# Token tile by token tile in the last two parts of four products, and mask matmuls ahead of the weighted products

## The reference

```python
# block 1: forgetting attention (8 heads), stick-breaking attention, a mixture of 16 experts
# block 2, layer 0:
m = concat(y_conv, y_mla) @ a_w_out                        # "aout"
x = x + rms_norm(m, norm_mix_post[0])
h = rms_norm(x, norm_mlp_pre[0])
x = x + rms_norm(relu(h @ w1[0])**2 @ w2[0], norm_mlp_post[0])   # "up0", "down0"
# block 2, layer 1: attention with 16 heads (compressed, selected, window branches)
m = mixer_c(rms_norm(x, norm_mix_pre[1]))                  # "cin", attention, "cout"
x = x + rms_norm(m, norm_mix_post[1])
x = x + rms_norm(relu(h @ w1[1])**2 @ w2[1], norm_mlp_post[1])   # "up1", "down1"
return x
```

## Time and profile before

| what | value |
|---|---|
| median of 3 runs | 2326.39 us (2326.12 to 2327.95) |
| the profiled execution's own time | 2325.24 us |
| its span | 2323.4 us |
| mean granted TensorE clock | 0.971 |
| TensorE matmul busy | 2192.1 us, 94% |
| VectorE busy / ScalarE busy | 1249.9 us, 54% / 942.8 us, 41% |
| chain that ended last | PE 83%, DVE 8%, DMA 4%, ACT 3%, issue 2% |
| joins: stretches | 1147.8 to 1171 (aout), 1509 to 1533 (down0), 1941 to 1965 (cout), 2303 to 2323.4 (down1) |
| first attention loop / second | 130 to 178 / 1684 to 1903 |

### The profile page before, as it was taken

How to read it: one execution, slowest core, us unless ns; L and a number is a source line. 1 busy time by engine, 2 the same in 40 slices (tenths; PEclk the granted TensorE clock), 3 DMA queues, 4 the chain that set the end, 5 groups by cost and what they waited for, 6 DMA issues and landing times.

```text
span 2323.4 us, 25971 instructions
## 1 busy us (share of the span) xinstructions
PE 2192.1 (94%) x10216; PEld 1689.6 (73%) x10216; DVE 1249.9 (54%) x1719; ACT 942.8 (41%) x1464; POOL 183.2 (8%) x228
## 2 busy tenths in 40 slices
PE   7999999979999968998999999989999998999998
PEld 4767678857666636886778888878766667888886
DVE  6745564468677735366554444453346666344444
ACT  4444542246555524335431134342255555112333
POOL 1230000202000010001000000020222200000000
PEclk9999999999999988999999999999899999999999
DMA  9404023939999972220232232242100002332231
GB/s 352 142 14 157 25 103 132 387 111 343 357 370 376 377 253 99 82 87 15 73 97 94 91 102 98 91 114 88 39 1 1 1 20 73 102 107 91 91 109 55
DMA packets 142951, 308.92 MB, mean 133 GB/s; under 512 B 12438, under 2 KB 14123, under 8 KB 142829
## 3 DMA queue, kind: packets, MB, share of 16 engines
q1 hardware_dynamic: 120484, 229.75, 28.8%
q0 software_dynamic: 11648, 41.60, 4.6%
q10 hardware_dynamic: 10700, 35.91, 4.5%
HBM read 276.04 MB, written 30.99 MB: 132 GB/s over the span
## 4 chain that ended last, share of the span: by engine, by line
PE 83%; DVE 8%; DMA 4%; ACT 3%; issue 2%; ACTq 0%; POOLq 0%; POOL 0%; SPq 0%; DVEq 0%
PE PB L1648 57%; PE PB L2134 5%; PE PB L2418 4%; DMA BIG<-in_expert_w_down 3%; PE PB L2390 1%; PE PB L2391 1%; DVE WL L2521 1%; PE PB L1797 1%; PE PB L1895 1%; PE PB L1776 1%; PE PB L2339 1%; PE PB L2365 1%; PE PB L2074 1%; DVE X L2581 1%; PE PB L1965 1%
## 5 line engine op out<-in xcount | busy, mean ns | idle before, releaser
L2521 DVE TENSOR_TENSOR WL<-RING,WH 128x1024 fp32r<-128x1024 f32 x232 | 288.4, 1243 | 622.6 <-ACT WH L920 400.5
L920 ACT CAST WH<-RING 128x1024 fp32r<-128x1024 f32 x232 | 243.5, 1050 | 792.9 <-PE PB L1648 786.6
L1648 PE MATMUL PB<-HTH,WH 128*128 128x512 f32 x1056 | 413.7, 392 | 8.7 <-DVE WL L2521 3.4
L1648 PE MATMUL PB<-HTL,WH 128*128 128x512 f32 x1056 | 412.4, 391 | 0.0
L1648 PE MATMUL PB<-HTH,WL 128*128 128x512 f32 x1056 | 412.1, 390 | 0.0
L1648 PEld LDWEIGHTS PB<-HTH,WH 128*128 128x128 f32 x1056 | 199.1, 189 | 52.5 <-issue 9.6
L1648 PEld LDWEIGHTS PB<-HTH,WL 128*128 128x128 f32 x1056 | 199.1, 189 | 41.8
L1648 PEld LDWEIGHTS PB<-HTL,WH 128*128 128x128 f32 x1056 | 199.4, 189 | 40.9
L1648 PE MATMUL PB<-WH,NHH 128*128 128x512 f32 x512 | 199.4, 389 | 1.8 <-DVE NHL L2524 1.8
L1648 PE MATMUL PB<-WL,NHH 128*128 128x512 f32 x512 | 199.2, 389 | 0.0
L1648 PE MATMUL PB<-WH,NHL 128*128 128x512 f32 x512 | 199.2, 389 | 0.0
(11 more groups left out here) (559 smaller groups left out, 3527.8 us busy)
## 6 DMA issues: line engine op xcount, KB each, us to landing
RING<-in_mlp_w SPq DMA_DIRECT2D x64, 1024.0 KB, 5.1
RING<-in_expert_w_gate SPq DMA_DIRECT2D x32, 1024.0 KB, 7.6
RING<-in_expert_w_up SPq DMA_DIRECT2D x32, 1024.0 KB, 11.9
BIG<-in_expert_w_down ACTq DMA_DIRECT2D x15, 2048.0 KB
RING<-in_w_in SPq DMA_DIRECT2D x20, 1024.0 KB, 5.5
BIG<-in_ada_w SPq DMA_DIRECT2D x9, 2048.0 KB, 14.7
dispatch_rows<-BIG POOLq DMA_DIRECT2D x24, 512.0 KB, 18.7
RING<-in_a_w_in SPq DMA_DIRECT2D x10, 1024.0 KB, 5.0
```

Source lines behind the costliest of these rows:

```text
L920: ins = nc.scalar.copy(weight_buffers(stage)[0][:, q % 2], halves_of(n, q))
L1648: yield pe.matmul(dst, lhs, rhs, start=(start and n == 0), stop=(stop_ and n == 2))
L2521: ins = V.tensor_tensor(wl, halves_of(n, q), wh.bitcast(F32), ALU.subtract)
```

## The change

- The last part of the four products gets buffers of its own (`LAST_BUFFERS`, in memory that is free then), so ScalarE no longer waits with its high half until the part before has begun. The parity of the weight buffers of up0 and down0 is turned (`W_PARITY`).
- The last two parts of the second group run tile by tile: tile b takes part 6 (or 30) and part 7 (or 31), 12 matmuls, then tile b+1. The last part's operands are waited for at tile 0.
- In the join, ScalarE squares row i-1 of `X` right behind the bank of tile i, and VectorE does for tile i the multiply, the reciprocal and the `X` update, and then the normed row of tile i-1. For down0 the normed rows go to `XN`, since the last parts' rows lie in the memory of `NAT`.
- In both attention loops the maximum masks stand right behind the score mask, ahead of the spread, the transposition of maxima and the weighted product.

```diff
--- before.py
+++ after.py
@@ -783,6 +783,14 @@
 
         BUFFERS = {"down0": (NHH, NHL), "down1": (NHH, NHL), "aout": (HTL[:, 0:4, :], HTL[:, 4:8, :])}
 
+        LAST_PART = {"aout": 7, "cout": 7, "down0": 31, "down1": 31}
+        W_PARITY = {"up0": 1, "down0": 1}
+        LAST_BUFFERS = {
+            "aout": over("LASTA", ht_at, [P, 4, 2, W], F32R), "cout": over("LASTC", big_at + 4096 * F, [P, 4, 2, W], F32R),
+            "down0": over("LASTD", htl_at, [P, 4, 2, W], F32R)}
+        LAST_BUFFERS["down1"] = LAST_BUFFERS["down0"]
+        JOINED = {"aout": NAT, "cout": NAT, "down0": XN}
+
         def weight_buffers(stage):
 
             return (CWH, CWL) if stage == "cout" else (WH, WL)
@@ -791,6 +799,18 @@
         def input_buffers(stage):
 
             return BUFFERS[stage] if stage in BUFFERS else (HTH, HTL)
+
+        def split_weights(stage, q):
+
+            if q == LAST_PART.get(stage):
+                return LAST_BUFFERS[stage][:, 0], LAST_BUFFERS[stage][:, 1]
+            return tuple(t[:, (q + W_PARITY.get(stage, 0)) % 2] for t in weight_buffers(stage))
+
+        def split_rows(stage, q):
+
+            if q == LAST_PART.get(stage):
+                return LAST_BUFFERS[stage][:, 2], LAST_BUFFERS[stage][:, 3]
+            return tuple(tiles_of(t, q % 2) for t in input_buffers(stage))
 
         INPUTS = {
             "wout": lambda q: tiles_of(MT, q % 4), "cout": lambda q: tiles_of(OTS[q % 4 // 2], q % 2),
@@ -883,12 +903,18 @@
                     nc.scalar.activation(SQ512, PB[4 + i][:, :], ACT.Square, accum_out=SSB[:, one]).then_inc(n_sq, 1)
                     act.wait_ge(n_sq, 2 * NT * k + NT + i + 1)
                     nc.scalar.activation(PRMS[:, one], SSB[:, one], ACT.Sqrt, bias=MSA[:, one], scale=1.0 / D).then_inc(p_rms, 1)
-                for i in range(NT if rows_again else 0):
-                    one = slice(i, i + 1)
-                    row_tiles[0] += 1
-                    act.wait_ge(x_rows, row_tiles[0])
-                    link(nc.scalar.activation(SQ1024, X[:, i, :], ACT.Square, accum_out=SS[:, one]))
-                    nc.scalar.activation(RMS[:, one], SS[:, one], ACT.Sqrt, bias=EPSC, scale=1.0 / D).then_inc(n_rms, 1)
+                    if rows_again and i > 0:
+                        row_squares(i - 1)
+                if rows_again:
+                    row_squares(NT - 1)
+
+            def row_squares(i):
+
+                one = slice(i, i + 1)
+                row_tiles[0] += 1
+                act.wait_ge(x_rows, row_tiles[0])
+                link(nc.scalar.activation(SQ1024, X[:, i, :], ACT.Square, accum_out=SS[:, one]))
+                nc.scalar.activation(RMS[:, one], SS[:, one], ACT.Sqrt, bias=EPSC, scale=1.0 / D).then_inc(n_rms, 1)
 
             row_tiles = [0]
 
@@ -915,14 +941,14 @@
 
                 act.wait_ge(arrived[n % SLOTS], slot_count(n, turn, chunks_a_turn))
 
-                if SPLIT[stage] + q > 1 and (stage, q) != ("aout", 1):
+                if SPLIT[stage] + q > 1 and (stage, q) != ("aout", 1) and q != LAST_PART.get(stage):
                     act.wait_ge(part_begun, part_no(stage, q, turn, parts_a_turn))
-                ins = nc.scalar.copy(weight_buffers(stage)[0][:, q % 2], halves_of(n, q))
+                ins = nc.scalar.copy(split_weights(stage, q)[0], halves_of(n, q))
                 if stage in INPUTS:
                     if stage in ("down0", "down1"):
                         m = GR["up" + stage[-1]] + q % 16 // 2
                         act.wait_ge(acc_free[m % 2], m // 2 + 1)
-                    ins = nc.scalar.copy(input_buffers(stage)[0][:, 2 * (q % 2):2 * (q % 2) + 2, :], INPUTS[stage](q))
+                    ins = nc.scalar.copy(split_rows(stage, q)[0], INPUTS[stage](q))
                 ins.then_inc(high_ready, 1)
 
             def evac(g, dst, func=ACT.Copy, scale=1.0, banks=4, width=T):
@@ -1650,14 +1676,15 @@
             def split_group(g, stage, q0, kind, parts=4, wait_norm=None, midway=None, midway_at=2, by_bank=False):
 
                 await_set(g)
-                x = input_buffers(stage)
-                for m in range(parts):
+                tail = by_bank and stage in LAST_PART
+                for m in range(parts - 2 if tail else parts):
                     q = q0 + m
                     pe.wait_ge(low_ready, part_no(stage, q) + 1)
-                    w = tuple(t[:, q % 2] for t in weight_buffers(stage))
+                    w = split_weights(stage, q)
+                    x = split_rows(stage, q) if kind == "D" else input_buffers(stage)
                     for b in range(4):
                         for k in range(2):
-                            kk = 2 * (q % 2) + k if kind == "D" else 2 * m + k
+                            kk = k if kind == "D" else 2 * m + k
                             if wait_norm is not None and (b == 0 or m == 0 and k == 0):
 
                                 pe.wait_ge(norm_low, wait_norm - ND + max(kk, b) + 1)
@@ -1672,7 +1699,27 @@
                             ins.then_inc(bank_done, 1)
                     if midway is not None and m == midway_at:
                         midway()
+                if tail:
+                    ins = last_parts_by_bank(g, stage, q0 + parts - 2)
                 ins.then_inc(acc_done, 1)
+
+            def last_parts_by_bank(g, stage, q0):
+
+                for b in range(NT):
+                    for q in (q0, q0 + 1):
+                        if b == 0:
+                            pe.wait_ge(low_ready, part_no(stage, q) + 1)
+                        w, x = split_weights(stage, q), split_rows(stage, q)
+                        for k in range(2):
+                            for n, ins in enumerate(three(PB[4 * (g % 2) + b][:, :], w, k, x, k, "D",
+                                                          slice(b * P, (b + 1) * P), False, q > q0 and k == 1)):
+                                if b == 0 and k == 0 and n == 0:
+                                    ins.then_inc(part_begun, 1)
+                                if b == 0 and k == 0 and n == 1 and q == q0:
+                                    begin(ins, None)
+                    if b < NT - 1:
+                        ins.then_inc(bank_done, 1)
+                return ins
 
 
             pe.sem_inc(acc_done, GR["mod"])
...
@@ -2447,14 +2494,14 @@
                             pe.wait_ge(q_ready, h + 3)
                         maxima(h + 2, *MAX_TURNS[t])
                     score_mask(n)
+                    if h + 2 < NSA_H and t < len(MAX_TURNS):
+                        max_masks(h + 2, *MAX_TURNS[t])
                     if h % 2 and h >= 3 and t in (1, 3, 5):
                         spread((h - 3) // 2, t // 2)
                     if h + 2 < NSA_H and t == PER_HEAD - 1:
                         max_T(h + 2)
                 if n >= 2:
                     weighted(n - 2)
-                if h + 2 < NSA_H and t < len(MAX_TURNS):
-                    max_masks(h + 2, *MAX_TURNS[t])
 
             def last_pair():
 
@@ -2517,11 +2564,11 @@
             def split(stage, q, n, turn, parts_a_turn, chunks_a_turn):
 
                 dve.wait_ge(high_ready, part_no(stage, q, turn, parts_a_turn) + 1)
-                wh, wl = (t[:, q % 2] for t in weight_buffers(stage))
+                wh, wl = split_weights(stage, q)
                 ins = V.tensor_tensor(wl, halves_of(n, q), wh.bitcast(F32), ALU.subtract)
                 if stage in INPUTS:
-                    rows, (high, low) = slice(2 * (q % 2), 2 * (q % 2) + 2), input_buffers(stage)
-                    ins = V.tensor_tensor(low[:, rows, :], INPUTS[stage](q), high[:, rows, :].bitcast(F32), ALU.subtract)
+                    high, low = split_rows(stage, q)
+                    ins = V.tensor_tensor(low, INPUTS[stage](q), high.bitcast(F32), ALU.subtract)
                 ins.then_inc(low_ready, 1)
 
             def normed_rows():
@@ -2564,28 +2611,31 @@
             def join(stage, rows_again=True):
 
                 k = POST.index(stage)
-                for i in range(NT + 3):
-                    if i < NT:
-                        dve.wait_ge(n_sq, 2 * NT * k + NT + i + 1)
-                        ins = V.tensor_tensor(MN[stage][:, i, W:D], PB[4 + i][:, :], ROW[:, W:D], ALU.mult)
-                        if i == NT - 1:
-                            ins.then_inc(acc_free[1], 1)
-                        else:
-                            link(ins)
-                    if 0 < i <= NT:
-                        one = slice(i - 1, i)
-                        dve.wait_ge(p_rms, NT * k + i)
-                        if i == NT:
-                            dve.wait_ge(acc_free[1], (GR[stage] + 1) // 2 + 1)
-                        link(V.reciprocal(PRSTD[:, one], PRMS[:, one]))
-                        V.scalar_tensor_tensor(out=X[:, i - 1, :], in0=MN[stage][:, i - 1, :], scalar=PRSTD[:, one],
-                                               in1=X[:, i - 1, :], op0=ALU.mult, op1=ALU.add).then_inc(x_rows, 1)
```

(31 more changed lines are left out.)

10 lines of the change are left out of this document (5 added, 5 removed).

## The result

The changed kernel takes 2307.29 us (median of 4 runs, 2306.50 to 2314.21) against 2327.17 us (4 runs, 2326.12 to 2334.31) for the kernel before, run beside it: ratio 0.9915, 95% interval [0.9887, 0.9942]. The forecast was 2308.5, with a range of 2303.5 to 2316.

A forecast was written before the change was run, and what follows sets the result against it. TensorE was taken as the bound: its waits in joins and its matmul stream in attention loops. Savings 12.3 + 2.8 - 2.3 + 5.1 = 17.9 us off 2326.39 gave 2308.5, range 2303.5 to 2316.

The forecast's parts named there:

- Joins: Behind aout, down0, cout: next stage's first product 8.4 us after E, the last product's end; 12.3 us saved in all.
- allowance of 0.3 us for slow transposes: In each join: tile 3's transposes delayed by earlier tiles' slow ones, moving E + 8.1 to E + 8.4.
- End: At the kernel's end: last `X` update starts sooner behind the last bank's square, 2.8 us saved.
- Wait for the last part: In four products TensorE waits for the last part's low half: 2 x 0.75 + 2 x 0.4 = 2.3 us given back.
- Masks in the second loop: Second attention loop: masks behind the score mask cost 0.053 us each, saving 4.1 us.
- The forecast's estimate by the same 81 ns: Both attention loops, at the Trainium skill's matmul price: about 1 us saved instead of 5.1, time about 2312.5.
- Masks in the first loop: First attention loop: 18 groups in the same order as the second loop, 1.0 us saved.
- (a): After three joins a lowered clock reaches into the next stage, 1.6 us each, 4.8 in all; about 2313; chance 0.17.
- (b): Attention loops: moved masks save nothing, or the weighted product's weight load is exposed; about 2315 us; chance 0.13.
- (c): Joins: ScalarE and VectorE in lockstep, bank squares waiting for `X` updates, 8.4 us given back; 2317; chance 0.05.
- (d): Last parts: wait for operands, moved forward, exceeds 5.05 us a stage; slower than before, 2330 at 6 us; chance 0.02.
- (e): Whole kernel: the change does nothing, 2326 us; chance 0.02.

The follow-up runs named there:

- experiment 5: The changed kernel run again, unedited: 2306.14 us, ratio 0.9913 to the kernel before.
- experiment 2: Changed kernel with ScalarE's four row squares again behind all four banks and VectorE staggered as before; tile-by-tile products kept: 2321.29 us.
- Experiment 3: Changed kernel with the last two parts run part by part again, own buffers and new join order kept: 2321.11 us.
- experiment 1: Changed kernel with the maximum masks back behind the weighted product in both attention loops: 2313.67 us.
- experiment 4: Changed kernel with the masks on the causal maxima made twice, 136 more bf16 matmuls of 128 columns: 2314.05 us.
- 8: Changed kernel with `X` updates ahead of normed rows, earlier low halves, and the first loop's masks back behind the weighted product: 2307.66 us.
- 5 to 8: Four runs; the one without its own line: changed kernel with low halves of the last parts ready earlier, 2308.60 us.
- experiment 6: Changed kernel with VectorE updating tiles 2 and 3 of `X` ahead of the normed rows of tiles 0 to 2: 2307.59 us.

## Why the prediction was right, and where not

**Joins: right.** Forecast E + 8.4 in each, measured E + 8.31, 8.31 and 8.02; saved 3.87, 3.88 and 5.13 = 12.9 us against 12.3. The allowance of 0.3 us for slow transposes fits aout and down0 of this profile (8.31 against 8.02 at full clock); in cout the clock was full and it wasn't needed, and in experiment 5's profile neither aout nor cout needed it. One reading was too coarse: in cout's old join not all transposes ran slowly, the clock was 0.50 at first and 0.71 over the last 3.1 us. Experiments 2 and 3 show what the forecast took as one thing and never priced apart: the tiles' order and the join's order need each other.

**End: right.** 2.86 us against 2.8.

**Wait for the last part: right in kind, a quarter too small.** The last 48 products got longer by 0.90, 0.55, 0.93 and 0.55 = 2.9 us against 2.3. The starts of the products itemise it. In aout the step from 1153.71 to 1154.73 is 1.02 us where a product takes 0.23, so the wait costs 0.79, as forecast; in the MLP-down products it costs 0.40, as forecast. But the first product behind each wait then takes 0.34 until the next begins instead of 0.23. These 0.11 us, four times, are the greater part of the 0.6 that the forecast lacks. (The bracket in the profile shows less, 0.63 and 0.2, because it counts from a product's modelled end.) Experiment 3 shows that all of it comes with the tiles' order.

**Masks in the second loop: right, and larger.** 4.7 us with heads 1 to 13 at 182.3 and 177.6; the forecast's 4.1 for 14 heads is 3.8 for these 13. The prices held (one mask 0.109 down to 0.056, doubled masks 0.056 each). Heads 1, 2 and 10 gain just the forecast's 4.1 / 14 = 0.29 us, the other even ones about 0.45 and the odd ones 0.58 to 0.66. Part of the surplus is a wait that I had not seen: from the second score matmul to the product for the compressed maxima TensorE took 0.31 us in odd heads and 0.16 in most even ones before, and takes 0.117 in every head but one now. Before, this product started 0.06 us behind the end of a reduction on VectorE, so it waited for that bank; now the reduction ends about 0.12 us or more ahead. The rest of the surplus is not itemised. Without head 8 the gain is 5.8 us. Against it stands the new wait there, 1.61 us in that place instead of 0.17:

```profile
1802.52 0.95 DVE L3383 RECIPROCAL CI<-SUMS 12x128 f32<-12x128 f32 x1 [2.01 <-DMA SUMS<-RST]
1803.48 0.76 DVE L3374 TENSOR_REDUCE MX<-PB 128x1 f32<-128x384 f32 x2
```

VectorE waits 2.01 us for a load of sums, the maxima behind it in its queue come late, and TensorE, now ahead of its former time, runs into it (1.3 us). The head took 14.79 us. In experiments 1 and 4, where TensorE runs later, the place takes 0.17 and 0.117. By the Trainium skill's 81 ns a matmul in such a stream (TensorE: Matmul & The Clock Gate, Back-to-back issue gap) 136 further masks would cost 11 us, an estimate; experiment 4 shows 6.8, and the measured 0.056 decides. The forecast's estimate by the same 81 ns comes out at 1.7 us saved and not at 1: 102 groups at 0.11 - 0.081, less 14 at 0.162 - 0.07.

**Masks in the first loop: wrong.** The step that failed is "the first loop has 18 groups and the same order: 1.0", and behind it two premises: that TensorE never idles in the attention loops, and that what waits for a weighted product has slack. The loop takes 30.22 us with the masks ahead and 30.15 without. This loop is not bound by TensorE's stream. TensorE and ScalarE from one head to the next in the changed kernel, and two rows of the kernel before:

```profile
151.85 0.49 PE L1942 MATMUL PB<-PROB,FV 128*128 128x128 f32 x2
...
152.37 0.58 ACT L1039 COPY FOT<-PB 64x512 f32<-64x512 f32 x1 [1.01 <-PE PB L1942]
...
153.81 0.86 PE L1942 MATMUL PB<-PROB,FV 128*128 128x384 f32 x2
153.97 0.58 ACT L1031 CAST FQA<-PB 4x512 fp32r<-4x512 f32 x1
...
154.69 0.47 PE L1928 MATMUL PB<-FQA,FKA 128*128 128x512 f32 x1
```
```profile
153.57 0.86 PE L1895 MATMUL PB<-PROB,FV 128*128 128x384 f32 x2
154.23 0.47 PE L1881 MATMUL PB<-FQA,FKA 128*128 128x512 f32 x1
```

A head's last weighted product releases the copy on ScalarE, behind it come another copy and an exponential, then the cast that the next scores wait for, and these start 0.14 us behind its end (153.97 + 0.58). In the kernel before the same steps lie as far apart (151.38, 151.91, 153.51, 154.23). TensorE's own stream between the two got shorter: from 151.85 to 153.81 it is 1.96 us, where it was 2.19. But the next scores now start 0.88 us behind 153.81, where they started 0.66 behind 153.57. What the masks save there comes back as a wait. The brackets do not show this wait, because the modelled end of the row at 153.57 (154.43) lies behind the scores' start; the missing bracket is what I had read as "never idles".

What counts is the rest of the cycle, from those scores to the weighted product that closes the head. One mask used to stand there (0.11), and two behind it, off the cycle. Now all three stand ahead of it, at 0.056 each. In heads 1, 2 and 4 this stretch got 0.05 us longer (3.15 to 3.21 in heads 2 and 4), in heads 3 and 5 0.05 shorter (3.26 to 3.21), in all 0.06 us. Experiment 4 agrees: of its four more masks a head three lie in that stretch, and the head grows by three prices, 0.16. So do 1 and 8 (masks back, 0.07 us less in five heads). That ScalarE's queue closes the cycle is read from the rows; no run shortened it.

**Sum.** 12.9 + 2.9 - 2.9 + 4.7 - 0.1 = 17.5 us, where I had 17.9. The errors went both ways and nearly cancelled. The medians differ by 19.9 us in this pair, with an interval from 13.5 to 26.3, so that 2308.5 and 2307.29 lie so close together is luck in part. One more difference between the profiles is in no term of mine. In the earlier trace rows cout's first half waits 2.12 us for a part and then runs at a clock of 0.52. In the changed kernel it waits 2.13 us in the same place and the clock stays full, in both profiles, which makes this half 1.6 us shorter:

```profile
1919.71:1923.21 3.50, 3.50 (x15) 2.92 (x16) 0.88 (x1) 2.00 (x2) 0.00 (x0) 1.00 0.02 5
```

Behind the same wait, the clock over 3.5 us is 0.52 in experiment 1, 0.60 and 0.70 in 4 and 3, and 1.00 in 2 and 5 to 8. Whether the edit brings this about or it falls so by chance is not shown.

**Rivals.** (a), the clock: in aout's join the windows below have it at 0.50 and then full ahead of the first product of the next stage (1172.86), and down0's are alike, so it costs the transposes something and the next stage nothing. In both profiles of this kernel the clock is 1.00 over the first 3.4 us of up0, cin and up1: refuted. But experiments 2, 6 and 8 have joins in which the transposes themselves are slow and cost 1.2 to 1.6 us, and in 2 the low clock reaches a little into up0 and cin (0.92 and 0.93 over their first 3.4 us). The windows of the changed kernel's join behind aout, then one of experiment 2:

```profile
1166.98:1170.40 3.42, 3.42 (x19) 3.42 (x18) 2.67 (x5) 1.44 (x3) 0.00 (x0) 0.50 0.00 0
1170.40:1172.86 2.46, 1.57 (x14) 1.36 (x13) 1.03 (x3) 1.61 (x3) 0.00 (x0) 1.00 0.00 0
1172.86:1176.30 3.44, 3.44 (x15) 2.88 (x16) 3.44 (x5) 3.44 (x7) 0.00 (x0) 1.00 0.43 92
```
```profile
1159.00:1165.20 6.20, 5.38 (x24) 5.00 (x25) 3.15 (x7) 2.84 (x6) 0.00 (x0) 0.50 0.00 0
```

(b), masks that save nothing: refuted by experiment 1, true of the first loop alone. (c), lockstep: refuted, in aout's join the squares of the banks start 0.03 to 0.09 us behind the banks' last products, and ScalarE is idle for 0.34 us ahead of the last one. (d), a wait of over 5 us: it costs 0.55 to 0.93. (e) is out by the result.

## What to carry to other kernels

When work of several tiles arrives faster than the engines behind it can finish a tile (1.36 us against 2.98 here), first change how the tiles arrive, and then let the consumers finish tile by tile; either change alone can be worth nothing. A matmul moved inside a loop is only worth its price if the loop is bound by that engine's stream: follow the cycle from one round to the next across all engines before counting instructions, since a step moved ahead of the cycle's link is paid in full there. And where runs of one program differ by ten microseconds, an edit of two has to be judged by its local distances.

## What was unexpected of the hardware

- Two profiles of the same kernel on one core differ by 12.8 us of span with equal work; 11.5 us of it lie where the granted clocks differ (0.970 and 0.976 over the span), mostly in stages the change doesn't touch. The runs of the changed kernel take 2301.4 to 2317.1 us.
- The joins came out at 8.00 us and at 9.52 within one execution of experiment 6: the idle times ahead of the transposes were the same, 1.55 and 1.27 us, but the 24 transposes took 2.84 us at full clock and 4.51 at a lowered one.
- Behind the same wait of 2.1 us in cout the clock over the next 3.5 us was 0.52 in two profiles, 0.60 and 0.70 in two others and 1.00 in six.
- At full clock the first product of 512 columns behind one of the new waits takes 0.34 us until the next begins, a later one 0.23.
- A bf16 mask of 128 columns costs 0.11 us between two float32 products and 0.056 behind another bf16 mask. Where the other 0.05 goes is not shown; the rows only say that it is paid once for a group.
